# Expert results written over the gathered rows: four row buffers in place of three and a result buffer

## What is computed

```python
def expert_step(acc, args):
    wg, wu, wd, cw = args
    hh = jax.nn.silu(x @ wg) * (x @ wu)
    return acc + (hh * cw[:, None].astype(hh.dtype)) @ wd, None

y, _ = lax.scan(expert_step, jnp.zeros_like(x), (w_gate, w_up, w_down, combine.T))
```

## Time and profile before

| | us |
|---|---|
| three runs: median (lowest to highest) | 1358.05 (1355.63 to 1359.54) |
| the profiled execution | 1351.79 |
| its span, first to last instruction | 1349.6 |
| ... experts: first gather issued to last result written | 930.07 to about 1289.6 |
| ... finish: from about 1300 to the end | 50 |
| mean granted PE clock, of 2.4 GHz | 0.941 |

### The profile page before, as it was taken

One profiled execution on the slowest core, in us unless ns is written; L12 is line 12 of the kernel. 1 busy time (PEld: TensorE's weight loads), 2 busy tenths in 40 slices (PEclk: granted clock), 3 DMA queues, 4 the chain that ended last, 5 costly groups with the idle time before them and its releaser, 6 DMA issues. The chain is left out here.

```text
span 1349.6 us, 19893 instructions
## 1 busy us (share of the span) xinstructions
PE 1161.5 (86%) x7175; PEld 767.0 (57%) x7175; DVE 518.6 (38%) x1320; ACT 342.2 (25%) x854; POOL 295.1 (22%) x233
## 2 busy tenths in 40 slices
PE   4688999999999999999886999951998999899846
PEld 2346888888888888888773555521333333333312
DVE  2432244444444444535533466653112121111118
ACT  4422233333332333333442222110101011111102
POOL 2031313030302121110002565533112221211001
PEclk9677999999999999999998999975999899999978
DMA  9771202020102121110130111115998999999646
GB/s 372 291 287 50 71 19 89 1 88 3 60 11 70 53 78 45 54 53 26 47 140 8 63 53 57 47 32 236 419 393 313 386 379 388 376 374 363 249 185 250
DMA packets 53538, 218.56 MB, mean 162 GB/s; under 512 B 9904, under 2 KB 26680, under 8 KB 42560
## 3 DMA queue, kind: packets, MB, share of 16 engines
q1 hardware_dynamic: 36912, 117.26, 23.7%
q10 hardware_dynamic: 7632, 82.05, 15.3%
q0 software_dynamic: 8896, 17.93, 3.4%
HBM read 196.62 MB, written 30.03 MB: 168 GB/s over the span
## 5 line engine op out<-in xcount | busy, mean ns | idle before, releaser
L729 PE MATMUL att_piece_ps<-hT_hi,w_hi 128*128 128x384 f32 (+1 forms) x528 | 185.2, 351 | 2.0 <-DVE att_k_lo_sb L857 0.8
L1595 PE MATMUL moe_gu_ps<-moe_a_gu_sb,moe_xT_sb 128*64 x416 | 184.4, 596 | 2.0 <-DVE moe_xT_sb L1737 2.0
L1598 PE MATMUL moe_gu_ps<-moe_b_gu_sb,moe_xT_sb 128*64 128x512 f32 x416 | 184.4, 596 | 0.0
L729 PE MATMUL att_piece_ps<-hT_hi,w_lo 128*128 128x384 f32 (+1 forms) x528 | 173.6, 329 | 0.0
L729 PE MATMUL att_piece_ps<-hT_lo,w_hi 128*128 128x384 f32 (+1 forms) x528 | 173.2, 328 | 0.0
L916 DVE COPY att_pT_sb<-att_pT_ps 128x512 f32<-128x512 f32 (+2 forms) x192 | 94.6, 521 | 134.0 <-PE att_pT_ps L790 133.4
L1200 PE MATMUL mix_y_ps<-mix_w_out_sb,mix_oT_sb 128*128 128x512 f32 (+1 forms) x288 | 127.2, 600 | 2.2 <-ACT mix_oT_sb L1268 2.2
L1595 PEld LDWEIGHTS moe_gu_ps<-moe_a_gu_sb,moe_xT_sb 128*64 128x64 f32 x416 | 57.2, 138 | 121.2 <-issue 121.2
L977 ACT ACTIVATE att_probs_sb<-att_probs_sb,att_nmax_sb 128x640 f32<-128x640 f32 (+5 forms) x144 | 101.2, 703 | 42.1 <-DVE att_nmax_sb L902 41.3
L902 DVE CUSTOM_DVE_ANT_0 att_probs_sb<-att_s_ps,att_bias_sb 128x640 f32<-128x640 f32 (+5 forms) x144 | 95.2, 662 | 26.8 <-PE att_s_ps L778 14.6
L729 PEld LDWEIGHTS att_piece_ps<-hT_hi,w_hi 128*128 128x128 f32 x528 | 99.8, 189 | 9.4 <-issue 4.7
(11 more groups left out here) (280 smaller groups left out, 1801.6 us busy)
## 6 DMA issues: line engine op xcount, KB each, us to landing
moe_b_gu_sb<-in_w_gu ACTq DMA_DIRECT2D x26, 2048.0 KB
moe_b_dn_sb<-in_w_dn ACTq DMA_DIRECT2D x26, 1024.0 KB
moe_a_gu_sb<-in_w_gu SPq DMA_DIRECT2D x10, 2048.0 KB
keep_rows_all_sb<-in_w_ada SPq DMA_DIRECT2D x8, 2048.0 KB, 12.2
att_w_raw_sb<-in_w_qkv SPq DMA_DIRECT2D x21, 512.0 KB, 3.3
moe_a_dn_sb<-in_w_dn SPq DMA_DIRECT2D x10, 1024.0 KB
in_w_ada_sb<-in_w_ada SPq DMA_DIRECT2D x4, 2048.0 KB, 11.5
in_x_sb<-in_x_prompt SPq DMA_DIRECT2D x8, 512.0 KB, 7.0
```

The costliest lines, as they stand in the source:

```text
L729: ins = pe.matmul(bank[:, 0:hi - lo], w[:, kind, kc, :], x[:, kc, lo:hi], start=(m == 0), stop=(m == 3 * NC - 1))
L1595: pe.matmul(gu_ps[p % 2][LANE[0], :], xT[:, c, LANE[0]], a_gu[:, bass.ds(slot, 1), c, :].rearrange("p a n -> p (a n)"), start=(c == 0), st ...
L1598: ins = pe.matmul(gu_ps[p % 2][LANE[1], :], xT[:, c, LANE[1]], b_gu[p % 3][:, c, :], start=(c == 0), stop=(c == NC - 1))
```

## The change

The tile `y` is gone. There are four row buffers `x[0]` to `x[3]`, and a step's results are written into the buffer that held its gathered rows, which PE has transposed by then. ACT and DVE no longer wait for the scatter of the step before. A gather into a buffer now waits until the scatter out of it has landed: the gather of step q waits for the scatter of q-4. POOL issues `gather_ahead(p + 3)` in `body(p)` ahead of the scatter of p, where it was `gather_ahead(p + 4)`; the gather of step 3 is issued with the first three. One more buffer is cleared in `mix_out`. The scatter, gather and listing of a step move the same bytes as before.

```diff
-                x=[route.sb(f"x{j}", [P, D]) for j in range(3)])
+                x=[route.sb(f"x{j}", [P, D]) for j in range(4)])
...
-        for j in range(3):
+        for j in range(4):
             pool.memset(route["x"][j][:, :], 0.0).then_inc(x_zeroed, 1)
...
-    y = s.sb("y", [P, D])
...
         for p in range(3):
             gather(p)
-        for p in range(3, 6):
+        listing(3)
+        gather(3)
+        for p in range(4, 6):
             listing(p)
         n = look(pool, T_ROUNDS, 0, 1, ROUNDS)
 
         def gather_ahead(p):
-            pool.wait_ge(xT_ready, p - 2)
+            pool.wait_ge(scattered, 16 * (p - 3))
             gather(p)
 
-        gather_ahead(3)
         listing(6)
 
         def body(p, n):
-            following(pool, p + 4, n, lambda: gather_ahead(p + 4))
+            if p:
+                following(pool, p + 3, n, lambda: gather_ahead(p + 3))
             pool.wait_ge(y_out_act, p + 1)
             pool.wait_ge(y_out_dve, p + 1)
-            pool.indirect_dma_start(k["yrows"], bass.IndirectOffsetOnAxis(ap=entry[:, p, 1:2], axis=0), y[:, :], None,
+            pool.indirect_dma_start(k["yrows"], bass.IndirectOffsetOnAxis(ap=entry[:, p, 1:2], axis=0), x[p % 4][:, :], None,
                                     bounds_check=2 * TOK - 1, oob_is_err=False).then_inc(scattered, 16)
             following(pool, p + 7, n, lambda: listing(p + 7))
...
             act.wait_ge(y_ready, p + 1)
-            if p:
-                act.wait_ge(scattered, 16 * p)
-            act.activation(y[:, 0:512], y_ps[:, 0:512], ACT.Copy, scale=entry[:, p, 2:3].bitcast(F32))\
+            act.activation(x[p % 4][:, 0:512], y_ps[:, 0:512], ACT.Copy, scale=entry[:, p, 2:3].bitcast(F32))\
                .then_inc(y_out_act, 1)
...
             dve.wait_ge(y_ready, p + 1)
-            if p:
-                dve.wait_ge(scattered, 16 * p)
-            dve.tensor_scalar(y[:, 512:1024], y_ps[:, 512:1024], entry[:, p, 2:3].bitcast(F32), None, ALU.mult)\
+            dve.tensor_scalar(x[p % 4][:, 512:1024], y_ps[:, 512:1024], entry[:, p, 2:3].bitcast(F32), None, ALU.mult)\
                .then_inc(y_out_dve, 1)
```

More of the change, by code:

```diff
@@ L1166, in _ @@
         pool.wait_ge(listed, 32 * (NT + 1))
-        pool.wait_ge(x_zeroed, 3)
+        pool.wait_ge(x_zeroed, 4)
     @block.tensor
@@ L1464, in experts @@
     listed = [s.sem(f"listed{j}") for j in range(4)]
-    gathered, scattered = [s.sem(f"gathered{j}") for j in range(3)], s.sem("scattered")
+    gathered, scattered = [s.sem(f"gathered{j}") for j in range(4)], s.sem("scattered")
     gu_ld, dn_ld = [s.sem(f"gu_ld{j}") for j in range(3)], [s.sem(f"dn_ld{j}") for j in range(2)]
@@ L1549, in gather @@
             pool.wait_ge(listed[p % 4], 16 * (p // 4 + 1))
-            pool.indirect_dma_start(x[p % 3][:, :], None, k["h2"], bass.IndirectOffsetOnAxis(ap=entry[:, p, 0:1], axis=0),
-                                    bounds_check=TOK - 1, oob_is_err=False).then_inc(gathered[p % 3], 16)
+            pool.indirect_dma_start(x[p % 4][:, :], None, k["h2"], bass.IndirectOffsetOnAxis(ap=entry[:, p, 0:1], axis=0),
+                                    bounds_check=TOK - 1, oob_is_err=False).then_inc(gathered[p % 4], 16)
         for p in range(3):
@@ L1581, in transpose_x @@
         def transpose_x(p):
-            pe.wait_ge(gathered[p % 3], 16 * (p // 3 + 1))
+            pe.wait_ge(gathered[p % 4], 16 * (p // 4 + 1))
             for c in range(NC):
-                ins = pe.transpose(xT_ps[:, c, :], x[p % 3][:, c * P:(c + 1) * P], ident)
+                ins = pe.transpose(xT_ps[:, c, :], x[p % 4][:, c * P:(c + 1) * P], ident)
             ins.then_inc(xT_ready, 1)
```

## The result

| | before, on the same chip | after |
|---|---|---|
| runs | 4 | 4 |
| median (lowest to highest), us | 1358.8 (1355.63 to 1364.28) | 1436.49 (1434.76 to 1440.02) |
| the profiled execution, and its span | 1351.79, 1349.6 | 1436.1, 1434.3 |
| mean granted PE clock | 0.941 | 0.909 |

The ratio is 1.056, with a 95% interval of 1.054 to 1.059. The kernel became slower, by 78 us where 32 were forecast, and the time lies above the range.

What follows compares the result with a forecast made beforehand. Before, one scatter in flight out of one buffer was taken to bound; after, the gather loop. Step 23's result, 997.1 + 21 x 14.6 = 1303.7 against 1271.24, adds 32.5 us: predicted 1390, range 1350 to 1415.

Steps and rivals of the forecast that it cites:

- The chosen chain: Experts' stage: scatter landing, gather four steps on, transposes, down, result, next scatter; two steps per turn, 14.6 us a step; chance 0.69.
- Faster: Rival: the gather loop does not bind, the step falls to 12.1 us of PE and DMA, 1338 us; chance 0.14.
- No difference: Rival: the gather's added wait is met about when reached, step 12.9 to 13.2 us, within 4 us of 1358; chance 0.09.
- In series: Rival: a step's gather and scatter share a queue without overlap, scatter landing 16.9, step 17.3, total 1447 us; chance 0.08.
- The clearing: Fourth buffer's clearing on POOL ahead of the experts: 0.9 us, hidden in 18.72 us of idling, so nothing.
- 2T: Experts' stage, the reuse loop over two steps of length T: G + S + 6.3 us, 29.7 before two corrections.
- G: Landing of the gather after its issue, priced by the scatter's median: 11.4 us, bounds 3.2 and 17.9.
- S: Landing of a scatter issued behind a gather under way, priced by the listing: 12.0 us, bounds 11.4 and 17.9.
- relief: Landings' share above 3.2 us each, 17.0 together, shrinks as a longer step spreads weights thinner: step 14.2, not 14.85.
- The clock: PE's clock falls after long waits, slowing transposes and down by 1.8 us per loop, 0.9 a step; half taken, 0.4.
- The early gain: Start of the experts: gather of step 3 goes 18 us earlier, result of step 2 at 997.1, 3.6 us gained.
- T: Length of a step in the experts' stage: 14.6 us against 13.16, range 13.3 to 15.75.

Runs made afterwards that it cites:

- e4_five_lead4: The changed kernel with five row buffers and the gather of p+4, not p+3, waiting for the scatter of p-1: 1379.62 us, ratio 1.016.
- e5_after_half_b: The changed kernel with lane b loading half of its weights and using that half twice: 1356.84 us, 80 us below the changed kernel.
- e8_after_busy_pe: The changed kernel with six dummy PE matmuls ahead of the row transposes of every even step from step 4 on: 1427.37 us, ratio 1.049.
- e1_two_y: The kernel before with a second result tile, results waiting for the scatter two steps back, gathers for none: 1333.3 us, ratio 0.979.

## Where the prediction was right, and where it was wrong

**Right: the mechanism.** The chosen chain is the one that binds, link by link: gather tied to the scatter four steps back, rows needed two results on, ACT's and DVE's scatter waits gone, PE waiting ahead of the transposes. Three rivals are out. *Faster*: the gathers bind. *No difference*: 1436 is not 1358. *In series*: a landing of 16.9 us for the scatter is not what is there (the median is 11.9, the longest 16.3), though its time, 1447, is the nearest of the four; its step of 17.3 us was nearly right (16.88), for a wrong reason: luck. What binds is the loop of reuse through two steps and not POOL's own sequence of waits: in after 11 scatters still wait for the result in the window shown (50.6 us), and the five measured terms below add up to the loop, while in `e4_five_lead4`, where the sequence does bind, results wait for POOL. The clearing cost nothing (POOL still idled for 18.1 us behind it), and the tail is unchanged (17.8 for 17.6 us).

**Wrong: the step, 14.6 forecast and 16.88 measured.** From the result of step 2 to that of step 23, whose last step is a short one, there are 349.3 us where 21 x 14.6 = 306.6 were forecast: 43 us, and with 3 more ahead of step 2 that is the 46 us by which the median lies above the forecast. The terms of 2T, with the measured ones as means over the ten turns of the loop from the result of step 2 to that of step 22 (landings by the trace's completion events):

| term of 2T | forecast | measured |
|---|---|---|
| G, landing of the gather | 11.4 | 11.4 |
| S, landing of the scatter | 12.0 | 13.1 |
| relief of both by a longer step | -1.3 | none |
| transposes, down, with the clock | 4.7 + 0.8 | 6.8 |
| write to scatter | 1.6 | 1.6 |
| landing of the scatter to issue of the gather | 0 | 0.8 |
| sum | 29.2 | 33.8 |

The measured sum is formed before rounding, and with the 0.04 us from a gather's landing to its transposes it is the mean of the loop, 33.76: no term is missing. Four terms were mis-sized, by 1.3 (relief), 1.1, 1.3 and 0.8 us:

- *The relief* is the step of the prediction that failed in kind. I spread the weights evenly over a longer step. The share did fall, even below the forecast (0.75 for 0.83), but landings did not get shorter where it counts: the loads come in bursts of two steps, the critical gather and scatter lie in the bursts, and the relief (odd gathers of 3.2 to 5.9 us) goes to the chain that has slack. An average share says nothing about a transfer that is released by the same event as the loads. (That bursts are the reason rests on the windows above and on `e5_after_half_b`; a run with the loads spread evenly was not made.) The same blindness let me expect 14 to 15 us for every step where they alternate between 11.7 and 22.
- *S* was 1.1 short. The row it was priced by, the listing behind a scatter, had one gather's worth of rows ahead of it; the guess upward was right, its size was not.
- *The clock* falls in every loop, not in half: after each wait of 5.5 to 9.8 us the transposes take 1.97 for 1.04 and the first matmuls 1.12 for 0.64. I had halved it because the forecast waits were 2 to 3 us; gathered into every second step they are long. `e8_after_busy_pe` gives part of it back.
- *The wake-up*, 0.8 us from the landing to the issue behind it (landing of the scatter of step 6 at 1086.5 by its completion events, gather at 1087.31), was left out: no row that I had read showed it.
- *The early gain* of 3.6 us did not come: the result of step 2 is 32.3 us behind that of step 0, as before (32.7), where 29.1 was forecast. It passes one turn of the same loop, where three of the terms were too small: 12.0 + 0.8 + 11.2 + 6.6 for 11.4 + 0 + 11.4 + 4.7. Nor did the gather of step 3 go 18 us earlier: it was issued 24.8 us behind the first gather, as before (958.71 - 933.92 and 954.92 - 930.07), since POOL waited 17.1 us for its listing. What left the queue ahead of the first scatter was the gather of step 4, and that scatter did land in 12.0 us, not 17.9.

The range ended at 1415, at a T of 15.75. The bounds in the rows went much further (S up to 17.9), and I left them to a separate rival with a chance of 0.08, as if a landing between 12 and 16.9 could not be. By the Trainium skill, page "DMA: Bandwidth & Descriptors", section "Anatomy of one DMA", the estimate for such a transfer was 2.8 us. The quiet ones (most took 3.2 to 4.2 us) come near it, and the ones beside loads, 9 to 18 us, do not, with a median of 21.7 in `e1_two_y`.

A term of before was slightly off as well: PE's floor is 11.7 us a step (the odd steps of after, most steps of `e1_two_y`), not 12.1, since the busy time of the earlier trace rows was one at a granted clock of 0.97, and 12.1 x 0.97 = 11.7.

## What to carry to other kernels

When a buffer is reused for in- and outgoing data, walk the whole circle (landing out, wake-up, landing in, compute, issue) and divide by the number of steps it spans, and price its transfers by landings in the traffic that the same event releases, not by the mean share. If the write-out of one step must not hold up the next, give the result a second tile: it removed the same wait for the space of one more tile and left the loads free (-2.1% where reuse in place gave +5.6%). Before moving an instruction on a queue, ask what it then stands behind: a swap of two issues cost 122 us here.

## What the runs showed of the hardware that was not expected

- Rows that an indirect DMA leaves out by its bounds are not free: bytes on POOL's queue fell from 12.49 to 9.62 MB, packets stayed (6088, 6160), and the landings of the even gathers fell only from 11.3 to 10.8 us.
- The same DMA of about 84 rows of 4 KB took 3.2 us to land in a pause of the loads, 11 to 13 in a burst, and 21.7 at the median in `e1_two_y`, where the engines were at 0.94 all through and the result tiles let two scatters be under way beside the gather; which of the two made it so long was not separated. With a third less to move in a step (`e5_after_half_b`) the median of the gathers was 5.5 us.
- A wait of 1.02 us left PE's clock up (transposes 1.09 us), one of 4.78 us did not (1.97), though 5.32 us of matmuls stood right ahead of the wait in both.
